# Token tiles transposed by a diagonal, gate weights asked for later, the pair list worked out after the first pair's rows, in a hybrid decoder step on one Trainium2 core

## The chip, the cores and the metric

The kernel is one launch on one NeuronCore of one Trainium2 chip. The metric is device microseconds from start to end of an execution. A profile of one execution by the hardware profiler comes beside the times.

## The reference

One layer of a hybrid decoder step over 536 tokens (16 meta tokens, 512 prompt tokens, 8 decode tokens), all in float32. Cut to what matters here:

```python
h = rms_norm(x, norm_mix)                      # x * rsqrt(mean(x*x) + eps) * g, 1024 wide
p = h @ w_in                                   # mlstm q,k,v,o, 8 gate columns, attention q,k,v
... mLSTM heads and differential attention heads ...
x = x + concat(heads) @ w_out
h = rms_norm(x, norm_ffn)
g_idx = argmax(softmax(h @ w_group + b_group))            # one of 4 groups
top_v, top_i = top_k(expert logits of that group, 2)      # two of its 8 experts
for e in range(32):
    act = silu(h @ w_gate[e]) * (h @ w_up[e])             # 1024 -> 256
    y  += gates[:, e] * (act @ w_down[e])                 # 256 -> 1024
out = rms_norm(x + y, norm_final)
```

## The kernel before, in words

Tokens lie in five tiles of rows: four of 128 prompt tokens, and one of 40 rows (`T4`) with the meta and decode tokens. A list `ORDER`, written out by the function `schedule`, gives the order of work items; each engine walks the same list and does its own part of each item, with semaphores between them. SyncE (SP) issues nearly all DMAs; ScalarE (ACT), VectorE (DVE) and GpSimd (POOL) each have their own strict order too.

The head. SP asks for token tiles 0 and 1 (512 KB each), the first block of `w_in` (2 MB), and the other tiles. ACT asks for `gmix`, and for the eight gate columns of `w_in` in two DMAs (lines 969 and 970) whose pieces are 16 bytes each, into `wg`; it then squares and sums each token tile (line 979). POOL turns the sum into the row's factor `rr` (lines 802, 804). DVE multiplies the whole tile by `rr` into `hn` (line 1371). TensorE (PE) transposes `hn` in eight 128-column pieces (item `xt`, line 1804), and DVE copies the result, times `gmix`, into `hT` (line 1235). The list begins with `xt` 0, `xt` 1, `acc dv 0` (eight k-steps of a 128x512 product, line 1867), then `xt` 2, `acc dv 1`, and so on, one tile's transposes between two products. After block `dv` come `dq` (line 1864), the item `gates` (line 1846, which needs `wg`), `dk`, `mqk` and the mixers.

The middle. For the channel mixer the tokens are gathered by expert. Items `rank` and `invert` find, by a chain of small DVE operations, the slots of the first three pairs of experts (`EARLY`), and POOL gathers their rows from the DRAM tensor `tok_rows` into `XG` (line 901). Item `order` then makes the full list of pairs; at its end `table_ready` lets SP look up the later experts, and twelve more small DVE operations (lines 1674 to 1686) work out where the later pairs' slots lie. DVE then does `rows_of(0)` (line 1719: copies the first pair's transposed rows, times `gffn`, into `xT`), `late_ids` (lines 1694 to 1702 and `place_rows`) and `late_rows`.

The experts. 32 experts are worked through as 16 pairs and one repeated turn (`TURNS`, 17 turns). Three sets of weight slots hold three pairs; 3 MB belong to one expert. In a turn PE multiplies by gate and up weights (`gate_up`, line 2132), transposes the next pair's rows (line 2124), multiplies by the down weights of the turn before (line 2145) and transposes the activations (line 2138). SP asks for a later pair's gate weights when `gate_filled` says that the set's gate weights were used (line 543 from `next_gate_up`), for its up weights after `gu_filled` (line 546), and for its down weights after `dn_filled` (line 549).

Of the kernel before, what the change touches and what calls it, by code (L numbers as in the profile page):

```python
# [7 lines left out]
D = 1024  # L8
# [7 lines left out]
H = 4  # L16
DQ = 64
DV = 128
NEXP = 32
# [3 lines left out]
KC = D // 128  # L23
# [10 lines left out]
NTILES = NT + 1  # L34


SLOTS = 64
# [12 lines left out]
NOROOM = 4096  # L50
# [163 lines left out]
def build(nc, x_prompt, x_sample, cache_k, cache_v, state_C, state_n, state_m, page_table, meta_tokens,  # L214
# [7 lines left out]
    with ctx:  # L222
# [3 lines left out]
        def sem(name):  # L226
            return ctx.enter_context(nc.semaphore(name))
# [73 lines left out]
        feat = {"dq": dqT, "dk": dkT, "mqk": mqkT}  # L301
        hn = [HO[:, 0, :], HO[:, 1, :]]

# [45 lines left out]
        sums_ready = sem("sums_ready")  # L349
        hn_ready = sem("hn_ready")  # L350
        act_step, dve_step, pool_step, sp_step = (sem(n) for n in ("act_step", "dve_step", "pool_step", "sp_step"))
# [96 lines left out]
        riota = sb("riota", [128, 128])  # L448
        piota = sb("piota", [128, NPAIRS])
        iscr = moflat[:, 0:128].bitcast(i32)  # L450
        eidx = sb("eidx", [128, 32])
# [506 lines left out]
        def _(act):  # L958
# [7 lines left out]
            act.dma_start(gmix[:, :], norm_mix[0].rearrange("(p k) -> p k", k=KC)).then_inc(gmix_in, 16)  # L966
            g = w_in[0].rearrange("(p k) n -> p k n", k=KC)[:, :, W_COLS["gates"]:W_COLS["gates"] + 8]
            act.wait_ge(wg_zeroed, 1)
            act.dma_start(wg[:, :, 0:H], g[:, :, 0:H]).then_inc(wg_in, 16)
            act.dma_start(wg[:, :, 32:32 + H], g[:, :, H:2 * H]).then_inc(wg_in, 16)  # L970

            act.wait_ge(ident_made, 1)
# [10 lines left out]
            for item in ORDER:  # L983
# [14 lines left out]
                elif kind == "acc":  # L998
                    b, m = item[1:]
                    after(act, item, "a%d" % (m % 2))  # L1000
                    src = PS["a%d" % (m % 2)]
# [208 lines left out]
        def _(dve):  # L1210
# [151 lines left out]
            for item in ORDER:  # L1362
                kind = item[0]
                if kind == "xt":
                    j = item[1]
                    n = nrows(j)

                    for i in ((0, 1) if j == 0 else (j + 1,) if j + 1 < NTILES else ()):
# [186 lines left out]
                elif kind == "logit":  # L1555
                    j = item[1]
                    n = nrows(j)
                    if j == 0:
                        link(v.memset(Lt[:, :, :], 0.0))
                        link(v.tensor_copy(trib, tri[:, :]))  # L1560
                        link(v.tensor_copy(onesb, ones[:, :]))
                        link(v.memset(e32[0], 1.0))
                        link(v.memset(MM[:, 160:192], 0.0))
                    dve.wait_ge(rsq, RSQ["wo", j, 1 if j < T4 else 0])
                    after(dve, item, "t")
                    v.scalar_tensor_tensor(Lt[0:n, j, :], PS["t"][0:n, 0:36], rr[0:n, 5 + j:6 + j], br[0:n, :],
                                           ALU.mult, ALU.add).then_inc(freed["t"], 1)
                elif kind == "rank":
# [33 lines left out]
                    for dst, o in ((M1, o1), (M2, o2)):  # L1602
# [27 lines left out]
                elif kind == "order":  # L1630
# [42 lines left out]

                    link(v.tensor_tensor(xs, xin, rest, ALU.subtract))
                    link(v.tensor_tensor(q, eidx[:, :], below, ALU.subtract))
                    link(v.tensor_scalar(u_, q, float(2 * FULL), 2.0, ALU.is_ge, ALU.mult))
                    link(v.tensor_tensor(q, q, u_, ALU.add))
                    link(v.scalar_tensor_tensor(pos, below, float(2 * FULL), q, ALU.add, ALU.subtract))
                    link(v.tensor_tensor(pos, pos, top, ALU.mult))
                    link(v.tensor_tensor(pos, pos, q, ALU.add))  # L1680

                    link(v.scalar_tensor_tensor(u_, xs, 2.0, below, ALU.add, ALU.subtract))
                    link(v.tensor_tensor(u_, u_, top, ALU.mult))
                    link(v.tensor_tensor(d2, u_, top, ALU.subtract))
                    link(v.tensor_tensor(d1, xs, u_, ALU.subtract))
                    link(v.scalar_tensor_tensor(d1, d1, float(NEXP + 1), pos, ALU.add, ALU.subtract))

# [29 lines left out]
            def rows_in(dst):  # L1717
                for half in range(2):
                    ins = v.tensor_tensor(dst[:, 4 * half:4 * half + 4, :],  # L1719
                                          bank[half][:, :].rearrange("p (k t) -> p k t", t=128),  # L1720
                                          gffn[:, 4 * half:4 * half + 4, None].to_broadcast([128, 4, 128]), ALU.mult)
                return ins
# [25 lines left out]

            rows_of(0)
            late_ids()  # L1750
            late_rows()
# [12 lines left out]
            def further_pair(i):  # L1764
                dve.wait_ge(xt_filled, i + STATIC)
                rows_in(xT[0]).then_inc(xt_evac, 1)
# [26 lines left out]
        def _(pe):  # L1793
            def transpose_rows(rows, item, j):
# [331 lines left out]

            def gate_up(gu, rows, w, due):
# [23 lines left out]
            def xt(i):  # L2151
                pe.wait_ge(xg_in[i % 2], 16 * (i // 2) + 16)
                if i:
                    pe.wait_ge(xt_evac, i)
                rows_out(XG[i % 2]).then_inc(xt_filled, 1)
# [14 lines left out]
            for i in range(STATIC):  # L2170
                s, n = i % 2, TURNS[i][0]
                w = 2 * (n % NSETS)
                pe.wait_ge(xt_evac, i + 1)
# [4 lines left out]
                gate_up(PS["t" if s else "p"], xT[s], w, 32 * (n // NSETS) + 32)  # L2178
                if i == 0:
# [12 lines left out]
            def further_pair(i):  # L2192
                pe.wait_ge(xg_in[0], 16 * i + 16 * ((STATIC + 1) // 2))
                rows_out(XG[0]).then_inc(xt_filled, 1)
                pe.wait_ge(xt_evac, i + STATIC)
                gate_up(PS["p"], xT[0], 0, 32 * i + 32 * ((PAIRS + NSETS - 1) // NSETS))
                pe.wait_ge(act_done, i + STATIC)
# [36 lines left out]
```

## Time and profile before

| | |
|---|---|
| median of 3 runs | 730.23 us (725.73 to 734.33) |
| the profiled execution, its own time | 722.13 us |
| its span, first to last instruction | 720.4 us |
| mean granted TensorE clock | 0.931 |
| PE busy | 612.6 us, 85% |
| DVE busy | 280.2 us, 39% |
| HBM read and written | 150.91 MB and 19.01 MB |

Times below are microseconds from the start of the span; durations are microseconds or, where so marked, ns. The profiled execution was quicker than the median of the timed ones by 8 us, so differences are worked out within it and then set on the median.

### The profile page before, as it was taken

How to read it: one execution, taken by the hardware profiler on the slowest of the kernel's cores; microseconds unless marked ns; L12 is line 12 of the kernel's file. 1: busy time of each engine (PE TensorE's matmuls, PEld its weight loads, DVE VectorE, ACT ScalarE, POOL GpSimd, SP SyncE). 2: the span in 40 equal slices, each digit the busy share in tenths (PEclk: the TensorE clock that was granted, in tenths of full speed). 3: DMA queues.
4: the chain of work that ended last, by engine and by line, in shares of the span. 5: the costliest groups of instructions: out<-in, count | busy, mean ns of one | idle time of the engine just before them, and what ended most of it. 6: DMA issues, size and time to landing. Idle time of an engine off the chain costs nothing.

```text
span 720.4 us, 8557 instructions
## 1 busy us (share of the span) xinstructions
PE 612.6 (85%) x3155; PEld 329.5 (46%) x3155; DVE 280.2 (39%) x615; ACT 139.3 (19%) x405; POOL 117.3 (16%) x195
## 2 busy tenths in 40 slices
PE   4999999898999898999999961899999877999700
PEld 2544344344545454555555541555556443554300
DVE  3220069422343333368976758512121211112046
ACT  3110052223233433321032010101010000101011
POOL 2340017200210101100022101111111111110023
PEclk9999999997999899999989975899999998999965
DMA  9643337813120300041019498799999999999674
GB/s 283 203 116 133 118 115 219 286 34 117 45 73 0 118 1 0 1 117 41 20 47 392 167 347 351 313 410 420 419 420 420 420 422 421 422 417 419 250 267 179
DMA packets 49378, 161.45 MB, mean 224 GB/s; under 512 B 16443, under 2 KB 17772, under 8 KB 36664
## 3 DMA queue, kind: packets, MB, share of 16 engines
q1 hardware_dynamic: 39624, 143.67, 51.8%
q0 software_dynamic: 7488, 17.19, 7.2%
q8 instruction: 26, 0.43, 0.2%
q10 hardware_dynamic: 2224, 0.04, 0.2%
q14 instruction: 16, 0.13, 0.0%
HBM read 150.91 MB, written 19.01 MB: 236 GB/s over the span
## 4 chain that ended last, share of the span: by engine, by line
PE 68%; DMA 14%; SPq 7%; DVE 6%; ACT 2%; issue 2%; POOL 1%; POOLq 0%; DVEq 0%; ACTq 0%
PE bank L1867 11%; PE bank L1864 10%; PE bank L2082 8%; PE bank_p L2132 6%; PE scores L2145 5%; DMA WS<-in_w_down_e 4%; DMA FT<-in_w_down_e 4%; PE bank_t L2132 4%; SPq L546 3%; PE bank_t L1881 2%; SPq L549 2%; PE bank_p L1990 2%; SPq L543 2%; PE scores L1958 2%; DMA WS<-in_w_in 2%
## 5 line engine op out<-in xcount | busy, mean ns | idle before, releaser
L1867 PE MATMUL bank<-WS,XHT 128*128 128x512 f32 x192 | 90.7, 621 | 1.3 <-DMA WS<-in_w_in 1.1
L1864 PE MATMUL bank<-XHT,WS 128*128 128x512 f32 x192 | 84.7, 597 | 0.3 <-PE bank_t L1881 0.3
L1867 PEld LDWEIGHTS bank<-WS,XHT 128*128 128x128 f32 x192 | 36.5, 199 | 43.7 <-issue 41.6
L1864 PEld LDWEIGHTS bank<-XHT,WS 128*128 128x128 f32 x192 | 35.8, 190 | 42.5 <-issue 42.3
L2132 PE MATMUL bank_p<-WS,XHT 128*64 128x256 f32 x288 | 45.4, 391 | 5.5 <-DVE XHT L1719 1.5
L911 POOL DMA_INDIRECT out_rows<-MVA,slot_ids x17 | 17.0, 1001 | 188.6 <-DVE MVA L1736 188.6
L2132 PE MATMUL bank_t<-WS,XHT 128*64 128x256 f32 x288 | 43.0, 381 | 2.0 <-DMA FT<-in_w_up_e 1.3
L802 POOL TENSOR_SCALAR rr<-ss 128x1 f32<-128x1 f32 (+3 forms) x25 | 7.8, 312 | 183.0 <-ACT XHT L1141 63.8
L2132 PEld LDWEIGHTS bank_p<-WS,XHT 128*64 128x64 f32 x288 | 27.8, 141 | 20.7 <-issue 4.0
L1736 DVE COPY MVA<-scores 128x512 f32<-128x512 f32 x17 | 11.8, 692 | 57.1 <-PE scores L2145 57.1
L2132 PEld LDWEIGHTS bank_t<-WS,XHT 128*64 128x64 f32 x288 | 26.4, 137 | 16.1 <-DMA FT<-in_w_up_e 1.8
L1478 DVE TENSOR_TENSOR scores<-scores,maskneg 128x256 f32<-128x256 f32 (+1 forms) x20 | 7.7, 383 | 63.1 <-PE scores L1961 63.1
L2082 PE MATMUL bank<-WS,FT 128*128 128x512 f32 x64 | 29.6, 606 | 0.0
L2145 PE MATMUL scores<-WS,FT 128*64 128x512 f32 x72 | 24.4, 675 | 6.1 <-DMA WS<-in_w_down_e 5.3
L2124 PE MATMUL bank<-ident,DVt 128*128 128x128 f32 x136 | 20.5, 296 | 10.4 <-DMA DVt<-tok_rows,slot_ids 10.4
L843 POOL DMA_INDIRECT MO<-in_cache_k,pages x16 | 17.6, 1102 | 68.9 <-DVE Sd L1432 51.3
L2082 PE MATMUL bank<-WS,XHT 128*128 128x512 f32 x64 | 28.7, 594 | 0.0
L1757 DVE TENSOR_TENSOR MVA<-DVt,bank_p 128x256 f32<-128x256 f32 x9 | 3.8, 422 | 62.9 <-ACT DVt L1182 62.9
L981 ACT ACTIVATE MVA<-scores 128x512 f32<-128x512 f32 x17 | 10.1, 597 | 87.2 <-PE scores L2145 87.2
L1757 DVE TENSOR_TENSOR MVA<-DVt,bank_t 128x256 f32<-128x256 f32 x8 | 3.4, 422 | 59.7 <-ACT DVt L1182 59.7
L804 POOL TENSOR_TENSOR rr<-rr,neghalf 128x1 f32<-128x1 f32 (+3 forms) x25 | 24.9, 995 | 2.1
L2124 PEld LDWEIGHTS bank<-ident,DVt 128*128 128x128 f32 x136 | 17.1, 196 | 16.2 <-issue 16.2
(421 smaller groups left out, 1025.5 us busy)
## 6 DMA issues: line engine op xcount, KB each, us to landing
WS<-in_w_gate_e SPq DMA_DIRECT2D x16, 1024.0 KB, 19.3
WS<-in_w_up_e SPq DMA_DIRECT2D x16, 1024.0 KB, 21.6
WS<-in_w_down_e SPq DMA_DIRECT2D x16, 1024.0 KB, 24.9
WS<-in_w_in SPq DMA_DIRECT2D x6, 2048.0 KB, 11.8
XHT<-in_w_gate_e SPq DMA_DIRECT2D x10, 1024.0 KB, 22.5
XHT<-in_w_up_e SPq DMA_DIRECT2D x10, 1024.0 KB, 24.7
XHT<-in_w_down_e SPq DMA_DIRECT2D x10, 1024.0 KB, 26.3
FT<-in_w_gate_e SPq DMA_DIRECT2D x6, 1024.0 KB, 23.4
```

The source lines that it names most:

```text
L543: sp.dma_start(Wgu[w][:, 0], w_gate_e[0, e].rearrange("(p k) n -> p k n", k=KC)).then_inc(gate_in[w // 2], 16)
L546: sp.dma_start(Wgu[w][:, 1], w_up_e[0, e].rearrange("(p k) n -> p k n", k=KC)).then_inc(up_in[w // 2], 16)
L549: sp.dma_start(Wdn[w], w_down_e[0, e].rearrange("(p f) n -> p f n", f=FC)).then_inc(dn_in[w // 2], 16)
L804: pool.tensor_tensor(dst, dst, neghalf[0:dst.shape[0], 0:n], ALU.pow).then_inc(rsq, 1)
L843: pool.indirect_dma_start(dst, None, cache[0].rearrange("n t h d -> (n t) (h d)"), bass.IndirectOffsetOnAxis(ap=pages[:, b * NPAGES + p:b ...
L911: pool.indirect_dma_start(out_rows, bass.IndirectOffsetOnAxis(ap=slot_ids[:, c, 1:2].bitcast(u32), axis=0), YO[s], None, bounds_check=2 * ...
L1864: mm = pe.matmul(PS[r][:, :], w[:, k, 128 * m:128 * (m + 1)], hT[:, k, 0:512], start=(k == 0), stop=(k == KC - 1))
L1867: mm = pe.matmul(PS[r][:, :], hT[:, k, 128 * m:128 * (m + 1)], w[:, k, :], start=(k == 0), stop=(k == KC - 1))
L2082: mm = pe.matmul(PS[b][0:n, :], rows[:, k, col(j):col(j) + n], blkslot[(6 + half) % 3][:, first + k, :], start=(k == 0), stop=(k == 3))
L2124: mm = pe.transpose(bank[k // 4][:, 128 * (k % 4):128 * (k % 4) + 128], src[:, k:D:KC], ident[:, :])
L2132: mm = pe.matmul(gu[64 * u:64 * u + 64, DE * g:DE * g + DE], rows[:, k, 64 * u:64 * u + 64], Wgu[w + u][:, g, k, :], start=(k == 0), stop= ...
L2145: mm = pe.matmul(Sps[64 * u:64 * u + 64, 0, 512 * half:512 * half + 512], act_t[:, f, 64 * u:64 * u + 64], Wdn[w + u][:, f, 512 * half:512 ...
```

## The change

1. `hn` is gone. DVE makes a 128x128 diagonal `rrdiag` (the identity times the rows' factors), and PE multiplies the raw tile `X` by it, piece by piece: an ordinary float32 matmul in place of a transpose, for all five tiles of item `xt`. The transposes of `rt` and of the experts stay as they are.
2. The two DMAs for `wg` are issued by ACT when it comes to `acc dq 1`, not at the start.
3. In `rank` two small DVE operations of the chain go (the offset `NOROOM` is folded into constants that two operations at `logit 0` make).
4. The twelve operations after `table_ready` become `pair_places`, called after `rows_of(0)`.
5. `rows_in` signals `xt_evac` after each of its two halves, and `gate_up` waits for the first half before k-step 0 and for the second before k-step 4. The waits that count `xt_evac` count twice as far.

```diff
-        hn = [HO[:, 0, :], HO[:, 1, :]]
+        rrdiag = [HO[:, 0, 128 * n:128 * n + 128] for n in range(2)]
...
+        early_rows, early_pairs = Wd[:, 0, 0:2 * EARLY], Wd[:, 1, 0:EARLY]
...
-            act.wait_ge(wg_zeroed, 1)
-            act.dma_start(wg[:, :, 0:H], g[:, :, 0:H]).then_inc(wg_in, 16)
-            act.dma_start(wg[:, :, 32:32 + H], g[:, :, H:2 * H]).then_inc(wg_in, 16)
...
+                    if (b, m) == ("dq", 1):
+                        act.wait_ge(wg_zeroed, 1)
+                        act.dma_start(wg[:, :, 0:H], g[:, :, 0:H]).then_inc(wg_in, 16)
+                        act.dma_start(wg[:, :, 32:32 + H], g[:, :, H:2 * H]).then_inc(wg_in, 16)
...
-                        v.tensor_scalar(hn[i % 2][0:n], X[0:n, i, :], rr[0:n, i:i + 1], None, ALU.mult).then_inc(hn_ready, 1)
+                        v.tensor_scalar(rrdiag[i % 2][0:n, 0:n], ident[0:n, 0:n], rr[0:n, i:i + 1], None, ALU.mult).then_inc(rrdiag_made, 1)
...
+                        v.tensor_scalar(early_rows[:, :], eidx[:, 0:2 * EARLY], float(SLOTS), float(-NOROOM), ALU.mult, ALU.add)
+                        link(v.tensor_scalar(early_pairs[:, :], piota[:, 0:EARLY], float(-NOROOM), None, ALU.add))
...
-                    link(v.scalar_tensor_tensor(early, eidx[:, None, 0:ne].to_broadcast([128, NTILES, ne]), float(SLOTS), early,
-                                                ALU.mult, ALU.add))
-                    link(v.tensor_scalar(early, early, float(-NOROOM), None, ALU.add))
+                    link(v.tensor_tensor(early, early, early_rows[:, None, :].to_broadcast([128, NTILES, ne]), ALU.add))
...
-                    link(v.tensor_scalar(slot_of, slot_of, float(NOROOM), None, ALU.add))
-                    place_rows(first_onehots, piota[:, 0:EARLY])
+                    place_rows(first_onehots, early_pairs[:, :])
...
+            def pair_places():
...   (the twelve operations, unchanged)
             rows_of(0)
+            pair_places()
             late_ids()
...
-                rows_in(xT[s]).then_inc(xt_evac, 1)
+                rows_in(xT[s])          # .then_inc(xt_evac, 1) on each half, inside
...
+                        if g == 0 and k % 4 == 0:
+                            pe.wait_ge(xt_evac, evacuated + (1 if k else 0))
...
-                        mm = pe.transpose(dst[:, 128 * k:128 * k + n], rows[0:n, 4 * half + k:D:KC], ident[0:n, 0:n])
+                        if scaled is None:
+                            mm = pe.transpose(out, src, ident[0:n, 0:n])
+                        else:
+                            mm = pe.matmul(out, src, scaled[0:n, 0:n], start=True, stop=True)
...
-                    pe.wait_ge(hn_ready, j + 1)
-                    transpose_rows(hn[j % 2], item, j)
+                    pe.wait_ge(rrdiag_made, j + 1)
+                    transpose_rows(X[:, j, :], item, j, rrdiag[j % 2])
```

## Rows read from the trace of the kernel before

**Rows 1.** The chain that ended last, in order of time: start us, us, what; head.

```profile
1.72 11.55 DMA WS<-in_w_in
13.31 8.77 PE bank L1867 x16
22.08 0.88 PE scores L1804 x8
22.96 6.87 PE bank L1867 x16
```

**Rows 2.** Timeline of the head: start, us, engine, line, what, [idle before <-releaser].

```profile
2.89 0.29 POOL L778 TENSOR_SCALAR_AFFINE_SELECT ident<-ident 128x128 f32<-128x128 f32 x1 [0.24 <-POOL ident L777]
...
3.80 1.28 ACT L973 ACT_TABLE_LOAD   x1 [3.80 <-issue]
...
7.62 0.75 DVE L1371 TENSOR_SCALAR XHT<-XHT,rr 128x1024 f32<-128x1024 f32 x1 [4.46 <-POOL rr L804]
...
8.52 3.65 PE L1804 MATMUL scores<-ident,XHT 128*128 128x128 f32 x16 [8.52 <-DVE XHT L1371]
```

**Rows 3.** DMA queues in the first 13.3 us: packets, MB, share of 16 engines.

```profile
q10 hardware_dynamic: 1091, 0.02, 4.9%
```

**Rows 4.** Groups of instructions, whole span, shapes apart: xcount | busy us, mean ns.

```profile
L1990 PE MATMUL bank_p<-DVt,WS 128*128 128x128 f32 x80 | 14.5, 316 | 0.0
...
L1975 PE MATMUL bank_t<-ident,WS 128*128 128x128 f32 x40 | 8.1, 308 | 0.0
```

**Rows 5.** The chain again: one head's product by the values, in mid-kernel.

```profile
267.25 1.10 PE bank_p L1990 x8
```

**Rows 6.** Groups on DVE, shapes apart: a 128x128 product with a column.

```profile
L1422 DVE TENSOR_SCALAR gda<-gda 128x128 f32<-128x128 f32 x1 | 0.2, 227 | 0.0
```

**Rows 7.** The tile wg: time of its two DMAs from issue to landing.

```profile
DMA to landing us min/median/max: 13.9/16.8/19.6
```

**Rows 8.** ACT's timeline in block dq, and the chain at the gates.

```profile
56.69 0.60 ACT L981 ACTIVATE FT<-bank 128x512 f32<-128x512 f32 x1 [6.64 <-PE bank L1864]
...
82.63 7.03 PE bank_t L1846 x16
```

**Rows 9.** DVE's timeline at rank and at the pair list.

```profile
434.34 0.18 DVE L1615 TENSOR_SCALAR MO<-MO 128x30 f32<-128x30 f32 x1
...
447.64 0.19 DVE L1674 TENSOR_TENSOR MO<-MO 128x32 f32<-128x32 f32 x1
...
450.13 0.19 DVE L1686 SCALAR_TENSOR_TENSOR MO<-MO 128x32 f32<-128x32 f32 x1
...
451.00 1.29 DVE L1719 TENSOR_TENSOR XHT<-bank,gffn 128x512 f32<-128x512 f32 x2 [0.68 <-PE bank L2124]
...
457.10 1.48 DVE L1349 TENSOR_TENSOR MVA<-riota,MO 128x1280 bf16<-128x1280 f32 x1
```

**Rows 10.** The chain from the first gather to the second turn.

```profile
440.25 8.56 DMA DVt<-tok_rows,slot_ids
...
452.34 9.41 PE bank_p L2132 x64
461.82 1.28 ACT L1182
...
465.20 7.13 PE bank_t L2132 x64
```

**Rows 11.** Busy time by stretch: us, PE, PEld, DVE, ACT, POOL, PEclk, DMA share, GB/s.

```profile
456.00:458.00 2.00, 2.00 (x18) 1.20 (x16) 1.93 (x5) 0.00 (x0) 0.00 (x0) 0.76 0.05 14
...
470.00:475.00 5.00, 5.00 (x38) 2.89 (x36) 1.71 (x3) 0.38 (x1) 0.00 (x0) 1.00 0.99 400
...
640.00:660.00 20.00, 20.00 (x162) 12.12 (x158) 2.90 (x6) 1.90 (x5) 3.02 (x3) 1.00 1.02 421
```

**Rows 12.** SP's issues of gate weights in the first two turns.

```profile
458.48 0.36 SPq L543 DMA_DIRECT2D WS<-in_w_gate_e  x1
...
469.07 0.85 SPq L543 DMA_DIRECT2D WS<-in_w_gate_e  x2
```

More of the change, by code:

```diff
@@ L349, in build @@
         sums_ready = sem("sums_ready")
-        hn_ready = sem("hn_ready")
+        rrdiag_made = sem("rrdiag_made")
         act_step, dve_step, pool_step, sp_step = (sem(n) for n in ("act_step", "dve_step", "pool_step", "sp_step"))
@@ L966, in _ @@
             act.dma_start(gmix[:, :], norm_mix[0].rearrange("(p k) -> p k", k=KC)).then_inc(gmix_in, 16)
-            g = w_in[0].rearrange("(p k) n -> p k n", k=KC)[:, :, W_COLS["gates"]:W_COLS["gates"] + 8]
-            act.wait_ge(wg_zeroed, 1)
-            act.dma_start(wg[:, :, 0:H], g[:, :, 0:H]).then_inc(wg_in, 16)
-            act.dma_start(wg[:, :, 32:32 + H], g[:, :, H:2 * H]).then_inc(wg_in, 16)
             act.wait_ge(ident_made, 1)
@@ L999, in _ @@
                     b, m = item[1:]
+                    if (b, m) == ("dq", 1):
+                        g = w_in[0].rearrange("(p k) n -> p k n", k=KC)[:, :, W_COLS["gates"]:W_COLS["gates"] + 8]
+                        act.wait_ge(wg_zeroed, 1)
+                        act.dma_start(wg[:, :, 0:H], g[:, :, 0:H]).then_inc(wg_in, 16)
+                        act.dma_start(wg[:, :, 32:32 + H], g[:, :, H:2 * H]).then_inc(wg_in, 16)
                     after(act, item, "a%d" % (m % 2))
@@ L1366, in _ @@
                     n = nrows(j)
+                    if j == 0:
+                        dve.wait_ge(ident_made, 1)
                     for i in ((0, 1) if j == 0 else (j + 1,) if j + 1 < NTILES else ()):
@@ L1672, in _ @@
                     v.nop().then_inc(table_ready, 1)
[L1674 to L1686, printed above, removed]
+            def pair_places():
+                one32, extra, key, key2, top, incl, below, rest, xin, xs, pos, d1, d2, q, u_ = e32
+                link(v.tensor_tensor(xs, xin, rest, ALU.subtract))
+                link(v.tensor_tensor(q, eidx[:, :], below, ALU.subtract))
+                link(v.tensor_scalar(u_, q, float(2 * FULL), 2.0, ALU.is_ge, ALU.mult))
+                link(v.tensor_tensor(q, q, u_, ALU.add))
+                link(v.scalar_tensor_tensor(pos, below, float(2 * FULL), q, ALU.add, ALU.subtract))
+                link(v.tensor_tensor(pos, pos, top, ALU.mult))
+                link(v.tensor_tensor(pos, pos, q, ALU.add))
+                link(v.scalar_tensor_tensor(u_, xs, 2.0, below, ALU.add, ALU.subtract))
+                link(v.tensor_tensor(u_, u_, top, ALU.mult))
+                link(v.tensor_tensor(d2, u_, top, ALU.subtract))
+                link(v.tensor_tensor(d1, xs, u_, ALU.subtract))
+                link(v.scalar_tensor_tensor(d1, d1, float(NEXP + 1), pos, ALU.add, ALU.subtract))
             def late_ids():
@@ L1718, in rows_in @@
                 for half in range(2):
[L1719 to L1722, printed above, removed]
+                    v.tensor_tensor(dst[:, 4 * half:4 * half + 4, :],
+                                    bank[half][:, :].rearrange("p (k t) -> p k t", t=128),
+                                    gffn[:, 4 * half:4 * half + 4, None].to_broadcast([128, 4, 128]),
+                                    ALU.mult).then_inc(xt_evac, 1)
             def rows_of(i):
@@ L1765, in further_pair @@
                 dve.wait_ge(xt_filled, i + STATIC)
-                rows_in(xT[0]).then_inc(xt_evac, 1)
+                rows_in(xT[0])
                 dve.wait_ge(silu_done, i + STATIC)
@@ L1793, in _, with transpose_rows @@
         def _(pe):
-            def transpose_rows(rows, item, j):
+            def transpose_rows(rows, item, j, scaled=None):
                 n = nrows(j)
@@ L1803, in transpose_rows @@
                     for k in range(4):
-                        mm = pe.transpose(dst[:, 128 * k:128 * k + n], rows[0:n, 4 * half + k:D:KC], ident[0:n, 0:n])
+                        src, out = rows[0:n, 4 * half + k:D:KC], dst[:, 128 * k:128 * k + n]
+                        if scaled is None:
+                            mm = pe.transpose(out, src, ident[0:n, 0:n])
+                        else:
+                            mm = pe.matmul(out, src, scaled[0:n, 0:n], start=True, stop=True)
                     if len(names) == 2 or half == 1:
@@ L2125, in rows_out, with gate_up @@
                 return mm
-            def gate_up(gu, rows, w, due):
+            def gate_up(gu, rows, w, due, evacuated):
                 for g, (loaded, done) in enumerate(((gate_in, gate_filled), (up_in, gu_filled))):
@@ L2153, in xt @@
                 if i:
-                    pe.wait_ge(xt_evac, i)
+                    pe.wait_ge(xt_evac, 2 * i)
                 rows_out(XG[i % 2]).then_inc(xt_filled, 1)
@@ L2172, in _ @@
                 w = 2 * (n % NSETS)
-                pe.wait_ge(xt_evac, i + 1)
                 if i >= 2:
@@ L2177, in _ @@
                     pe.wait_ge(ids_ready, 2)
-                gate_up(PS["t" if s else "p"], xT[s], w, 32 * (n // NSETS) + 32)
+                gate_up(PS["t" if s else "p"], xT[s], w, 32 * (n // NSETS) + 32, 2 * i + 1)
                 if i == 0:
@@ L2194, in further_pair @@
                 rows_out(XG[0]).then_inc(xt_filled, 1)
-                pe.wait_ge(xt_evac, i + STATIC)
-                gate_up(PS["p"], xT[0], 0, 32 * i + 32 * ((PAIRS + NSETS - 1) // NSETS))
+                gate_up(PS["p"], xT[0], 0, 32 * i + 32 * ((PAIRS + NSETS - 1) // NSETS), 2 * i + 2 * STATIC - 1)
                 pe.wait_ge(act_done, i + STATIC)
```

## The prediction

> **What bounds the kernel now.** I read the chain of waits in order of time first, to see which waits stand where the change works, then the timeline and the DMA queues there, and last the busy time by stretch. PE is TensorE throughout. In the head the chain runs over the landing of the first `w_in` block: asked for at 1.72, it lands at 13.27, and `acc dv 0` starts at 13.31 and takes 8.77 us, where the same sixteen instructions take 6.87 us in the next product [rows 1]. From 22.08 on the chain is PE without a gap, transposes and products in turn, so what PE gains or loses in the head goes to the end of the router, through waits that PE itself sets off. In the middle the chain is the small DVE operations of `rank`, the gather of the first pair (8.56 us), its transposes, one evacuation and the first `gate_up` [rows 9, 10]. From 459 on the DMA queue is what counts. It stands idle from 456 to 458 (share 0.05), and from SP's issue at 458.48 on it runs at 0.99 to 1.02 of its time, about 421 GB/s, up to the last down weights [rows 11]. So after 459 PE's own time is worth nothing, and the end moves by as much as the issue at 458.48 moves, which is released by the gate half of turn 0 [rows 12].
>
> **The change part by part.**
>
> *Diagonal, tiles 2 to 4 (a loss).* An ordinary float32 product is two PE instructions where a transpose is one: the product by the values has 10 blocks and 4 heads, 40 calls, and shows 80 instructions; the transposes of the same 40 blocks show 40 [rows 4]. Eight instructions of 128 columns take 0.88 us as transposes [rows 1] and 1.10 us as parts of ordinary products, the first one's start-up in it [rows 5]. A tile goes from 8 instructions to 16, so it costs 0.88 us more (1.10 at most). Tiles 2, 3 and 4 stand in the gapless stretch: 3 x 0.88 = 2.64 us more, up to 3.3. Nothing hides it; DVE's 0.75 us for `hn` that goes is hidden there already.
> The Trainium skill ("TensorE: Matmul & The Clock Gate", section "Terms") has the transpose mode 4 times faster for float32; here the rows give 2 times. By the page each tile would cost three times 0.88 us more, not once.
>
> *Diagonal and gate weights, tiles 0 and 1 (a gain).* Today ACT loads its table for 1.28 us from 3.80, behind its two wg issues, then squares tile 0, and PE starts at 8.52 [rows 2]. Without the issues the table load can start once POOL's identity is there, at 3.2 to 3.3 [rows 2], so tile 0 is squared about 0.5 us sooner (between 0, if the tile's landing sets it, and 1.1 us, if the load doesn't wait for the identity). DVE's 0.75 us [rows 2] becomes a 128x128 product, 0.23 us [rows 6]: 0.5 us. PE starts at about 7.4. It then has 32 instructions, not 16; at the 228 ns of today (3.65 / 16 [rows 2]) they end at 14.7, later than today's 12.17.
> But the clock moves too. Sixteen instructions take 8.77 us in `dv 0` and 6.87 after it [rows 1]; at 429 ns each, doubled while the clock is at 1.2 GHz, 1.9 us too much means that it rose 3.8 us after the products began. Turn 0 takes 9.41 us against 7.13 [rows 10]: by the same sum it rose about 4.6 us after they began (granted 0.76 of full speed over 456 to 458 [rows 11]). If the diagonal products, which are ordinary ones, count the same, the clock is at 2.4 GHz 3.8 to 4.6 us after 7.4, at 11.2 to 12.0. By 11.6 PE has done 18.6 of the 32; 13.4 x 0.110 = 1.5 us more, and it is ready at 13.1.
> The block's landing: the wg pieces took 4.9% of the engines' first 13.3 us [rows 3], 0.65 us, so it lands at about 12.6 (12.6 to 13.3). The later of the two is 13.1. From there `dv 0` takes 6.87 and ends at 20.0, not 22.08: 2.1 us gained. Bounds: 2.6 gained (landing 12.6, clock up), 1.4 lost (ready at 14.7, 8.77 as today: ends at 23.47).
> The same page ("Part 4: PE-mode transpose") says that transposes do not count as busy for the clock gate. The sixteen transposes before `dv 0` did not leave a raised clock behind them [rows 1, 2], which fits; if they did count, the diagonal brings the clock nothing, and the first rival below is the case.
> Head in sum: 2.64 - 2.1 = 0.55 us slower.
>
> *wg later, at the gates.* ACT issues both behind the eviction of `dq 0`, at 57.3; it has nothing else until 63 [rows 8], so nobody queues behind it. The longest landing of before is 19.6 us, in a crowded queue [rows 7]: 57.3 + 0.8 + 19.6 = 77.7, and PE comes to the gates at 82.63 [rows 8]. Cost nothing, with 4.9 us of cover.
>
> *rank.* Two operations go, L1615 (0.18 us [rows 9]) and its like at L1618, with 0.03 to 0.04 us to the next start: 0.41 us off the chain to the gather. The gather takes 8.56 us and shares its queue with weights, so 0 to 0.41 comes through; DMA was nearly idle at its end, I take 0.41. The two added operations at `logit 0` run in a stretch where DVE waits for PE: nothing.
>
> *Half signals.* PE starts turn 0 after the first half of the evacuation, 1.29 / 2 = 0.65 us sooner. With rank 1.06 us sooner in all, at the low clock: if the clock then rises just as much sooner, 1.06 us reach the issue at 458.48; if it rises at the same moment as today, half, 0.53. I take 0.8. In later turns the evacuation lies beside the down product: nothing.
>
> *pair_places moved.* It brings no gain: today DVE has done the twelve operations at 450.32 and waits until 451.00 for PE's transposes [rows 9], so `rows_of(0)` wasn't held up. It costs its 2.68 us (447.64 to 450.32) in `late_ids`. Today that ends its one-hots at 457.10 + 1.48 = 458.58 [rows 9]; now at 458.58 + 2.68 - 0.41 = 460.9, with a gap or two more 461.0. PE ends turn 0's `gate_up` at 461.75 today (452.34 + 9.41 [rows 10]), now at 460.7 to 461.2. So PE's search for the later rows waits 0.3 us at most, DVE's slot ids come about when the first SiLU does (ACT loads a table for it, 1.28 us [rows 10]), and turn 1 starts near 464.1 against 465.20 [rows 10]. That is off the DMA chain: the wait is covered by the queue's work.
>
> **Sum.** +2.64 - 2.1 - 0.8 = -0.25 us on the profiled execution's 722.13: 721.9. The median of before is 8.1 us above that execution; set on it, 730.0 us. About 1% (7.3 us) is what a measurement of this kernel can tell from no change, and this is far inside.
>
> **The rivals.**
> 1. *The diagonal does not raise the clock sooner (slower).* PE is ready at 14.7 and `dv 0` takes 8.77 again: +1.4 + 2.64 - 0.8 = +3.2, 733.5 us. For it: the clock stayed low through the transposes before `dv 0`, and what counts for its rise shows only with wide products here. Against: turn 0's products have half the array's columns each and raised it. It decides as soon as the rise comes after 14.7.
> 2. *All of the head's gain comes (faster).* `dv 0` at 12.6, 1.06 us through to the queue, and turn 1's earlier gate weights fill the small gap at 470 to 475 (400 against 421 GB/s, 0.25 us [rows 11]): -2.6 + 2.64 - 1.06 - 0.25 = -1.3, 728.9 us.
> 3. *The later pair list surfaces.* Turn 1 waits for `ids_ready`, and SP's issue at 469.07 waits for turn 1's gate half. The 4 MB asked for from 458.48 on last 10 us at 421 GB/s, to about 468.6, so a later issue there leaves the queue empty. It decides when turn 1 starts after 465.2, 1.1 us later than worked out; at most 2.68 - 1.1 = 1.6 us, 731.6 us.
> 4. *The change does not do what it says at the gates:* wg lands over 25 us after its issue and PE waits there, some 1 us: 731.
> 5. *A plain product costs four transposes.* By rows as a mechanism: 64 instructions in tiles 0 and 1, ready at 11.6 + 45.4 x 0.11 = 16.6, `dv 0` ends at 23.5 (+1.4), tiles 2 to 4 cost 7.9: +8.5 with the middle's gain, 738.7. The counts in [rows 4] speak against it. The skill's page on TensorE is cited for this above.
>
> **How the numbers follow.** Forecast 0.45, its own range 729.2 to 731; rival 1 0.22, rival 2 0.17, rival 3 0.06, rival 4 0.03, rival 5 0.03, something else 0.04. The cases that hold most lie between 728.9 and 733.5. Three runs of one kernel spread from 725.73 to 734.33, which is wider than all terms here together, so a median of a few runs may lie 3 us off: 725.5 to 735. Faster by over 1% needs something not seen here: 0.03. Slower by over 1% is rival 5 and a part of the unknown: 0.05. Within 1%: 0.92.
>
> **What would show it.** L1804's successor shows 16 instructions a tile for `xt` at 110 to 137 ns each. The first product starts near 13.1, takes 6.9 us and ends near 20; if it takes 8.8, rival 1 is right. PE reaches `dq` 0.5 us later than 49.54, and the gates without a wait for wg. The first gather is issued at the same distance less 0.4 us from the last logit. Turn 0 starts about 0.65 us after its evacuation began. The twelve operations stand behind the evacuation, and PE waits under 0.3 us for the one-hots. SP's first gate issue of turn 0 comes about 0.25 us sooner than 458.48. The prediction is wrong if the gather or a landing in the decode part answers to the shift by more than the shift itself, or if the DMA stage is not bound by its bytes.

## The result: 1.5% slower, outside the predicted range

| | before | after |
|---|---|---|
| median of the runs on one chip, us | 730.01 (718.12 to 734.33, 22 runs) | 738.73 (728.53 to 745.13, 22 runs) |
| ratio, 95% interval | | 1.0154 (1.0108 to 1.0199) |
| profiled execution, its span, us | 722.13, 720.4 | 736.17, 734.3 |
| PE busy us, mean granted clock | 612.6, 0.931 | 627.2, 0.929 |

730.0 (725.5 to 735) was forecast; the medians lie 8.7 us apart. The medians here and below are over all runs of a kernel, the ratios over its fast runs alone (those within 1.5% of its fastest), so a ratio can differ from that of the medians: 1.0154 is 11.2 us. The head of the changed kernel's chain of waits, in order of time (start us, us, what), answers to [rows 1]:

```profile
0.79 3.44 DMA XHT<-in_x_prompt
4.31 1.16 ACT WS L975 x2
...
7.06 7.89 PE scores L1814 x32
14.95 6.87 PE bank L1877 x16
21.82 3.68 PE scores L1814 x16
...
42.91 3.92 PE scores L1814 x16
46.84 8.73 PE bank L1877 x16
55.57 3.61 PE bank_t L1891 x32
59.47 27.71 PE bank L1874 x64
...
92.55 7.03 PE bank_t L1856 x16
```

Read it downwards. The products by the diagonal (L1814) start at 7.06, 1.46 us sooner than the transposes of [rows 2], and `acc dv 0` takes 6.87 us, not 8.77: the clock is up when it begins (the trace's first record of full clock stands at 12.6, before at 16.6; ahead of a trace's first record its clock column reads 1.00 and says nothing). It begins at 14.95, though, not 13.31, since the 32 products before it last 7.89 us. Then each of tiles 2 to 4 takes 3.68 to 3.92 us where eight transposes took 0.88 to 1.00. The line at 46.84 is a third thing: `dv 3` takes 8.73 us, where 7.06 were taken before. Stretch by stretch (window, its length, busy time of each engine, granted clock, DMA share, GB/s), the clock fell right behind tile 4:

```profile
43.00:46.80 3.80, 3.80 (x17) 3.75 (x17) 0.00 (x0) 0.55 (x1) 0.00 (x0) 0.99 0.00 0
46.80:50.50 3.70, 3.70 (x6) 1.67 (x6) 3.11 (x12) 0.00 (x0) 1.95 (x2) 0.55 0.16 18
50.50:55.50 5.00, 5.00 (x13) 1.90 (x11) 0.77 (x4) 0.00 (x0) 3.26 (x11) 1.00 0.72 198
```

The account up to `dq`, which starts at 59.47 against 49.54: `dv 0` ends 0.26 sooner (21.82 against 22.08); tiles 2 to 4 cost 2.80, 2.80 and 2.92 more, 8.52; `dv 3` at the low clock costs 8.73 - 7.06 = 1.67. Together +9.93, which is the whole distance. The gates stand at the same +9.92, with no wait for wg.

The middle, on the same chain, answers to [rows 9, 10]:

```profile
442.83 0.26 DVE Lt L1571
...
455.38 8.54 DMA DVt<-tok_rows,slot_ids
...
466.03 1.29 DVE XHT L1724 x2
```

And PE's timeline there ([idle before <-releaser]):

```profile
466.87 0.66 PE L2144 MATMUL bank_p<-WS,XHT 128*64 128x256 f32 x1 [0.87 <-DVE XHT L1724]
...
476.38 0.42 PE L1822 MATMUL bank_t<-MVA 128*128 128x48 bf16 x10 [0.86 <-DVE MVA L1350]
```

Before, the last logit stood at 427.27, so the gather came 12.98 us behind it; now 12.55: 0.43 sooner. Turn 0 follows the start of its evacuation by 0.84 us, not 1.34, and stands 1.04 us nearer to the last logit. PE waits 0.86 us for the later rows' one-hots.

So the profiles show +9.93 at `dq` and -1.04 at turn 0: +8.9, beside 8.7 between the medians and 11.2 by the ratio. Between `dq` and the last logit this execution lost 5.6 us more; the experiments say whose those are.

### The profile page after: what moved, and what is told of

Its sections match the earlier page's. It is cut to its first block, busy times and chain, and to the rows that moved or that the text cites. A ratio compares the mean times of both kernels' runs of the same rounds, so it can differ in the third digit from the quotient of the medians.

```text
span 734.3 us, 8636 instructions
## 1 busy us (share of the span) xinstructions
PE 627.2 (85%) x3195; PEld 344.7 (47%) x3195; DVE 277.6 (38%) x615; ACT 139.3 (19%) x405; POOL 115.1 (16%) x195
## 3 DMA queue, kind: packets, MB, share of 16 engines
HBM read 150.91 MB, written 19.01 MB: 231 GB/s over the span
## 4 chain that ended last, share of the span: by engine, by line
PE 63%; DMA 12%; SPq 11%; DVE 7%; issue 2%; ACT 2%; POOL 1%; POOLq 0%; DVEq 0%; ACTq 0%
PE bank L1877 11%; PE bank L1874 10%; PE bank L2092 8%; SPq L547 4%; DMA WS<-in_w_down_e 4%; DMA FT<-in_w_down_e 4%; SPq L550 4%; PE scores L2157 3%; PE bank_p L2144 3%; PE bank_t L2144 3%; SPq L544 3%; PE scores L1814 3%; PE bank_p L2000 2%; PE bank_t L1891 2%; PE scores L1968 2%
## 5 line engine op out<-in xcount | busy, mean ns | idle before, releaser
L1877 PE MATMUL bank<-WS,XHT 128*128 128x512 f32 x192 | 92.4, 630 | 0.1
L844 POOL DMA_INDIRECT MO<-in_cache_k,pages x16 | 16.6, 1039 | 80.7 <-DVE Sd L1435 54.0
L2092 PE MATMUL bank<-WS,XHT 128*128 128x512 f32 x64 | 28.7, 594 | 0.0
L2157 PE MATMUL scores<-WS,MK 128*64 128x512 f32 x72 | 23.6, 624 | 2.7 <-DMA FT<-in_w_down_e 2.7
L2157 PE MATMUL scores<-WS,FT 128*64 128x512 f32 x72 | 21.9, 597 | 4.6 <-DMA WS<-in_w_down_e 3.8
L1814 PE MATMUL scores<-XHT 128*128 128x128 f32 (+1 forms) x80 | 19.6, 412 | 7.1 <-DVE XHT L1374 7.1
## 6 DMA issues: line engine op xcount, KB each, us to landing
WS<-in_w_in SPq DMA_DIRECT2D x6, 2048.0 KB, 11.3
```

Of the source, the lines that this page charges most:

```text
L844: pool.indirect_dma_start(dst, None, cache[0].rearrange("n t h d -> (n t) (h d)"), bass.IndirectOffsetOnAxis(ap=pages[:, b * NPAGES + p:b ...
L1814: mm = pe.matmul(out, src, scaled[0:n, 0:n], start=True, stop=True)
L1877: mm = pe.matmul(PS[r][:, :], hT[:, k, 128 * m:128 * (m + 1)], w[:, k, :], start=(k == 0), stop=(k == KC - 1))
L2092: mm = pe.matmul(PS[b][0:n, :], rows[:, k, col(j):col(j) + n], blkslot[(6 + half) % 3][:, first + k, :], start=(k == 0), stop=(k == 3))
L2157: mm = pe.matmul(Sps[64 * u:64 * u + 64, 0, 512 * half:512 * half + 512], act_t[:, f, 64 * u:64 * u + 64], Wdn[w + u][:, f, 512 * half:512 ...
```

## The experiments

Theory A, held from here on: an ordinary float32 product whose operand has its columns eight numbers apart, as `rows[0:n, 4 * half + k:D:KC]` has, costs about 230 ns for 128 columns (3.68 / 16) and not the 110 ns of the transposes, and this is the loss. Rivals: every ordinary product on tiles costs it (rival 5 of the prediction), the middle costs it, or the clock does.

**e1: the products by themselves.** Groups of ordinary products (two instructions each) and of transposes, behind wide products that hold the clock at full speed. It computes nothing of the step.

```
for k in range(16): pe.matmul(out, A[:, k % 8:1024:8], ident, ...)     # L290; L281: contiguous
for k in range(16): pe.transpose(out, A[:, k % 8:1024:8], ident)       # L299
for k in range(16): pe.matmul(out, ident, A[:, k % 8:1024:8], ...)     # L305: the moving operand
```

> A kernel of its own that computes nothing of the step: TensorE alone, groups of sixteen 128x128 float32 operations behind eight 128x512 products each. Ordinary products by the identity with the stationary operand's columns 1, 2, 4, 8 and 16 floats apart; transposes with the same operand contiguous, 8 and 16 apart; and products with the identity stationary and the moving operand 8 apart and contiguous. Theory A (the column step of the stationary operand of an ordinary float32 product sets the time): 110 to 115 ns an instruction at step 1, 230 at step 8, with the step from one to the other somewhere between; transposes 110 at every step; the moving operand's step costs nothing. Theory B (an ordinary product of a token tile by a 128x128 square is slow in any layout): 230 ns at step 1 too, or at least over 180.

Its timeline on PE:

```profile
15.75 3.73 PE L281 MATMUL q<-ident,A 128*128 128x128 f32 x32
...
36.82 7.50 PE L287 MATMUL q<-ident,A 128*128 128x128 f32 x32
...
51.03 7.65 PE L290 MATMUL q<-ident,A 128*128 128x128 f32 x32
...
65.39 7.04 PE L293 MATMUL q<-ident,A 128*128 128x128 f32 x32
...
79.13 1.91 PE L296 MATMUL q<-ident,A 128*128 128x128 f32 x16
...
87.75 1.94 PE L299 MATMUL q<-ident,A 128*128 128x128 f32 x16
...
105.06 7.62 PE L305 MATMUL q<-A,ident 128*128 128x128 f32 x32
```

and the groups of two of its lines, for the loads of the stationary operand (PEld) and the products (xcount | busy us, mean ns of one):

```profile
L290 PEld LDWEIGHTS q<-ident,A 128*128 128x128 f32 x32 | 7.8, 334 | 0.4 <-issue 0.2
...
L305 PEld LDWEIGHTS q<-A,ident 128*128 128x128 f32 x32 | 6.6, 207 | 1.2 <-issue 0.5
...
L281 PEld LDWEIGHTS q<-ident,A 128*128 128x128 f32 x32 | 3.7, 192 | 0.5 <-issue 0.5
```

Divide each group by its count: step 1 gives 117 ns, step 2 (3.92 us for 32) 122, step 4 (L287) 234, step 8 (L290) 239, step 16 (L293) 220. The transposes take 119 contiguous, 121 at step 8 and 123 at step 16. Theory A holds, with one miss: I had expected the moving operand to be free of it, and it costs 238 ns too. The loads suggest that the price sits in the instruction that reads the wide-stepped tile: the load takes 334 ns instead of 192 in L290, and 207 in L305, where the stationary operand is contiguous. In the changed kernel the loads of L1814 take 335 ns (median), in e5 192.

**e3 and e2: the diagonal alone, and everything but the diagonal.** e3 is the kernel before with the diagonal's edits; e2 is the changed kernel with the scaled copy and the transposes back:

```diff
-                        v.tensor_scalar(rrdiag[i % 2][0:n, 0:n], ident[0:n, 0:n], rr[0:n, i:i + 1], None, ALU.mult).then_inc(rrdiag_made, 1)
+                        v.tensor_scalar(hn[i % 2][0:n], X[0:n, i, :], rr[0:n, i:i + 1], None, ALU.mult).then_inc(rrdiag_made, 1)
...
-                    transpose_rows(X[:, j, :], item, j, rrdiag[j % 2])
+                    transpose_rows(hn[j % 2], item, j)
```

> The kernel before with part 1 alone. If the diagonal products are the loss: 8 to 11 us slower than before, ratio 1.011 to 1.015, dq starting 8 us or more later than 49.5. If the loss came from an interplay with the other parts: under 4 us slower.

> The changed kernel with part 1 undone: the scaled copy hn and transposes, all else of the change kept. If the diagonal products are the whole loss (3 x 2.8 us in tiles 2 to 4, 8.4 us in all): the gate weights' absence from the head, the shorter rank chain and the half signals are left, 1 to 2.5 us faster than the kernel before: ratio 0.9965 to 0.999. If something else in the change costs (pair_places later, gate weights later): slower than before by over 2 us.

e3 took 740.74 us against 726.97, ratio 1.0237 (1.0168 to 1.0306); e2 725.67, ratio 1.0028 (0.9991 to 1.0065). The loss goes with the diagonal: it is there in e3 and not measurable in e2. Neither ratio fell into the expected range, though. e2 should have come out faster than before and did not; by its interval up to 0.65% could still be the other parts'. e3 lost 13.8 us and not 8 to 11, 5 more than the changed kernel. It lacks that kernel's two gains: PE starts at 8.07, not 7.06, and turn 0 stands as far behind the last logit as before. That is 2 us; the other 3 are open. e3's chain has the same three things, the low clock behind tile 4 too:

```profile
8.07 7.89 PE scores L1810 x32
...
22.82 3.68 PE scores L1810 x16
...
43.92 3.93 PE scores L1810 x16
47.84 8.76 PE bank L1873 x16
```

In e2, `dv 0` is the line to read, from PE's timeline:

```profile
7.55 3.65 PE L1810 MATMUL scores<-ident,XHT 128*128 128x128 f32 x16 [7.55 <-DVE XHT L1372]
13.15 7.13 PE L1875 MATMUL bank<-WS,XHT 128*128 128x512 f32 x16 [1.95 <-DMA WS<-in_w_in]
```

There are only transposes ahead of it, as in the kernel before, and yet it takes 7.13 us, not 8.77: the first record of full clock stands at 11.2 in this trace, where the transposes end. So `dq` comes at 47.76, 1.8 us sooner than before, of which 0.16 is the earlier start and the rest the clock. Its turn 0 stands 1.05 us nearer to the last logit. Neither shows in its time.

**e4 and e5: the same products on neighbouring columns.** e4 is the changed kernel, reading 128 neighbouring columns of `X`. The features then stand in another order than the weights' rows, so the step's numbers are others:

```diff
+                        if scaled is not None:
+                            src = rows[0:n, 128 * (4 * half + k):128 * (4 * half + k) + 128]
```

> The changed kernel, but the pieces of X that PE multiplies by the diagonal are 128 neighbouring columns, not every eighth: the features come out in another order, so the numbers computed are others; sizes and counts are the same. Theory A: an instruction of L1814 takes 110 to 115 ns, a tile 1.8 us in place of 3.7, dq starts 5.5 us or more sooner than in the changed kernel, about level with the kernel before (ratio 0.997 to 1.003, as predicted blind). Theory B: no difference from the changed kernel, ratio 1.012 to 1.018. The routing of tokens changes with the numbers, so the expert stage may differ a little.

Its head did what was expected (1.78 us a tile, `dq` at 50.41), but its time, 767.92 us, ratio 1.0598, tells nothing: with other numbers the router chose other experts, and more was to be loaded and computed (157.72 MB read from HBM, not 150.91). e5 mends that by loading `w_in`, the gate weights and `gmix` in the same order, `"(k p) n -> p k n"` in place of `"(p k) n -> p k n"`, so that it computes the same thing as the reference.

> The changed kernel with the features dealt to the partitions the other way round: piece k of X is its 128 neighbouring columns, and the blocks of w_in, the gate weights and gmix are loaded to match, so the result is the reference's. Sixteen instructions a tile as in the change, stationary columns next to each other. Theory A (the step of 8 floats in an ordinary float32 product is what costs): a tile takes 1.8 us, dq starts within 1.5 us of 49.5, the whole within 3 us of the kernel before (ratio 0.996 to 1.004), 8 to 12 us faster than the changed kernel. If the diagonal costs for another reason that the bench does not have: ratio above 1.01.

725.95 us against 724.28, ratio 1.0013 (0.9973 to 1.0054). Its chain:

```profile
7.29 6.38 PE scores L1816 x32
13.67 6.87 PE bank L1879 x16
20.54 1.78 PE scores L1816 x16
...
37.84 1.91 PE scores L1816 x16
39.75 7.06 PE bank L1879 x16
...
50.71 27.70 PE bank L1876 x64
```

With the step gone, each of tiles 2 to 4 costs 0.90 us more than as transposes, `dq` stands 1.17 us later than before, and no low clock follows tile 4. This is the kernel that the blind sum described.

**e8: the diagonal for tiles 0 and 1 only,** where PE would otherwise wait for the weights; tiles 2 to 4 as scaled copies and transposes.

> The changed kernel with the diagonal for tiles 0 and 1 alone, transposes of a scaled copy for tiles 2 to 4. The 8.4 us of the three later tiles go; dv 0 starts near 15 as in the changed kernel but at the high clock, so dq starts near 49.3, 1.5 us later than with transposes throughout. Ratio to the kernel before 0.997 to 1.002. If it stays above 1.01, the loss is not in the later tiles' products.

```profile
15.21 6.87 PE bank L1883 x16
22.07 0.88 PE scores L1815 x8
...
38.58 7.06 PE bank L1883 x16
...
49.55 27.70 PE bank L1880 x64
```

`dv 0` starts 1.90 us later and takes 1.90 less: `dq` stands at 49.55, as in the first profile of before (49.54). Against that profile the whole loss of the head comes with the products of tiles 2 to 4, the low clock behind tile 4 included. Ratio 0.997 (0.9923 to 1.0016), as expected.

**e6, e7, e11: the middle in parts.** e6 is the kernel before with the changes to `rank`, the half signals and the pair list. e7 is e2 with the pair list back ahead of `rows_of(0)`. e11 is the kernel before with the pair list alone moved (`pair_places()` behind `rows_of(0)`).

> The kernel before with parts 3, 4 and 5 alone (shorter rank chain, pair_places later, half signals). Theory A: first gate issue of turn 0 comes 0.8 to 1.8 us sooner after the last logit, head unchanged; ratio 0.997 to 0.999. Rival (the moved pair list surfaces): turn 1 starts later after the last logit than before and the ratio is above 1.001.

> Transposes kept, parts 2, 3 and 5 kept, pair_places put back before rows_of(0). The twelve operations then stand where DVE waits over 3 us for PE's transposes; turn 0 starts as soon and the search for the later rows no longer waits (0.9 us in the changed kernel). If that wait reached the DMA queue: up to 1 us faster than with the list moved; if not, the same. Against the kernel before: ratio 0.995 to 1.001.

> The kernel before with part 4 alone: the twelve operations of the pair list behind the evacuation of the first pair's rows. By the blind sum it is neutral: the evacuation starts at the same distance from the last logit (within 0.1 us), PE waits 0 to 0.9 us for the later rows' one-hots, SP's first gate issue keeps its distance from the last logit, ratio 0.997 to 1.003. Rival 3 (the later list surfaces): turn 1 starts later by 1.1 us or more against turn 0, the queue falls empty before turn 1's gate weights, ratio 1.001 to 1.003 and the share of the DMA engines dips between turn 0 and turn 1.

| | us | against before | turn 0 from the last logit |
|---|---|---|---|
| e6 | 726.95 | 1.0049 (1.0018 to 1.008) | -1.25 us |
| e7 | 724.45 | 0.9995 (0.9952 to 1.0038) | -0.79 us |
| e11 | 728.94 | 1.0017 (0.9954 to 1.008) | -0.34 us |

The list moved alone costs nothing that can be seen: the distance between turns 0 and 1 grew by 0.21 us, not by the 1.1 from which rival 3 decides, and the DMA engines are at 1.00 of their time from 465 to 471.9, where turn 1's weights are asked for. The gain of the middle is in the profiles of e6 and e7, but in no ratio. e6 was expected to be faster (0.997 to 0.999) and comes out a little slower, which is open. Its ratio is the one named for the rival, but turn 1 doesn't start later, as the rival wants: it stands 36.12 us behind the last logit, 37.93 before. The profile has `dv 0` at 10.07 us, with the first full clock at 19.8, in a head that was not edited.

**e9 and e10: both kernels once more,** for what belongs to a run.

> The kernel before once more, with a profile of its own, to see which differences between two profiles come from run to run. If the stretches in which the granted clock is low between the block dq and the mixers' end belong to the run and not to the kernel, they lie elsewhere than in the first profile (171 to 181, 242 to 249, 365 to 372, 416 to 423 us) and add up to 3 to 8 us of shift at the last logit. If they belong to the kernel, they stand within 1 us of the same places. Either way dv 0 starts at 13.1 to 13.4 and no low stretch stands at 40 to 51 us.

> The changed kernel once more. Theory A (the step of eight in the products is the whole loss): each of tiles 2 to 4 again takes 3.6 to 3.9 us, dq starts 8 us or more after that of before. The drop of the clock after tile 4's products (from 47.0 in the first profile) stands again within 1 us if it belongs to these products; if it was a run's chance it is absent, and dq starts at 57.6 instead of 59.5. The last logit comes 8 to 10 us later than in the kernel before if the further 6 us of the first profile were drops of the run.

e10's chain in the head repeats that of the changed kernel to 0.05 us:

```profile
42.94 3.96 PE scores L1814 x16
46.90 8.68 PE bank L1877 x16
...
59.48 27.70 PE bank L1874 x64
```

So the drop of the clock behind tile 4 belongs to the kernel. The clock in `dv 0` is the run's, as long as transposes stand ahead of it. e9, whose `dv 0` starts at 13.68 and not at the expected 13.1 to 13.4, had it up at 11.3 and lost it again within `dv 0`, from 14.8 on:

```profile
15.10:18.50 3.40, 3.40 (x6) 1.34 (x5) 1.18 (x2) 2.27 (x4) 0.74 (x2) 0.55 1.07 260
```

Over all profiles of this study with transposes there, `dv 0` took 8.77 (before), 8.83 (e9), 10.07 (e6) and 7.13 us (e2, e7 and e11); with the diagonal at step 8 6.87 us in each of four (after, e10, e3, e8), with contiguous columns 7.13 and 6.87 (e4, e5).

What comes after `dq` differs by the run too. From `dq` to the last logit the kernel before took 377.7 us in its first profile and 384.6 in e9 (49.99 to 434.60), the changed kernel 383.4 and then 376.2. One kernel differs from itself there by 7 us. The places of the low clock are neither within 1 us of the first profile's nor altogether elsewhere: counted from `dq`, four of its five come again 1 to 8 us later in e9, one does not, and two are new. The clock is low for 31.8 us of this stretch in the first profile and 41.0 in e9 (mean granted 0.96 and 0.95), for 37.7 and then 23.9 in the changed kernel (0.95 and 0.97). At half clock at most half of such time is lost, so this covers 4.6 of the 6.9 us and 6.9 of the 7.2; the rest is open. The 5.6 us that the first pair of profiles had there are therefore not shown to be an effect of the change. Over all profiles this stretch took between 374.9 (e5) and 387.5 us (e4). That places e9 correctly as well: 729.92 us, with nothing changed, 7.8 above the first profiled execution.

**e12: narrower tiles, and the steps between.** Like e1; L281 has a stationary step of 3, L284 and L287 a moving step of 2 and 4, L290 and L293 products of 40 rows and 40 columns at step 8 (tile 4's shape), L296 the same contiguous; L274 are the wide products between, 7.03 to 7.05 us at full clock. It computes nothing of the step.

> It computes nothing of the step: ordinary float32 products by themselves on TensorE, each group behind eight wide products. Theory A (one operand whose columns lie 16 bytes or more apart costs double): stationary operand with step 3: 112 to 120 ns an instruction; moving operand with step 2: 112 to 120; with step 4: 225 to 235. Rival (the moving operand pays at any step): step 2 at 150 ns or more. Last, 40 rows by 40 columns with a stationary step of 8, as tile 4 has it: if few rows make it cheaper, below 150 ns an instruction; in the changed kernel they took 245. If such products do not hold the clock up, the granted clock falls behind the long run of 96 of them and the wide products after it take about 859 ns instead of 429; if the drop in the changed kernel had another cause, it stays at full speed.

```profile
15.69 5.68 PE L281 MATMUL q<-ident,A 128*128 128x128 f32 x32
...
38.57 7.41 PE L287 MATMUL q<-A,ident 128*128 128x128 f32 x32
...
52.79 7.83 PE L290 MATMUL q<-ident,A 40*128 40x40 f32 x32
60.54 9.82 PE L274 MATMUL acc<-B 128*128 128x512 f32 x16
70.29 23.05 PE L293 MATMUL q<-ident,A 40*128 40x40 f32 x96
93.27 8.82 PE L274 MATMUL acc<-B 128*128 128x512 f32 x16
102.02 3.76 PE L296 MATMUL q<-ident,A 40*128 40x40 f32 x32
105.71 8.83 PE L274 MATMUL acc<-B 128*128 128x512 f32 x16
```

Step 3 takes 178 ns, which theory A had at 112 to 120: the price comes in two steps, at 3 and at 4, and not at 4 alone. A moving step of 2 takes 118 (3.79 us for 32), of 4 232, as expected. The 40x40 products take 245 ns at step 8, as many as the full tile, and 118 contiguous. The wide products behind each 40x40 group are slow (9.82, 8.82, 8.83 us against 7.05), behind the contiguous group too: behind these small products the clock falls, whatever their step. And by stretch of the clock:

```profile
60.50:70.30 9.80, 9.80 (x18) 0.72 0.01 2
70.30:93.30 23.00, 23.00 (x98) 0.55 0.00 0
```

The 96 products ran at 240 ns each with the clock granted at 0.55: half TensorE's clock made the stepped products no slower. What limits them here is not TensorE's clock.

## Why the prediction was wrong

**The step that failed** is the first term, "Diagonal, tiles 2 to 4 (a loss)", where it took 0.88 us a tile, "1.10 at most". It measured 2.80, 2.80 and 2.92: 8.5 us and not 2.64. The count of instructions was right (16 for 8). The price of one was taken from the transposes of the same tile and from [rows 5], where both operands are contiguous. Neither row bounds an ordinary product that reads columns eight apart: transposes do not pay for the step (e1) and the rows of [rows 5] have none. The upper bound of 3.3 us came from a row that shared the shape and the type, but not the access. 5.9 us of the miss are here. With 1.8 us in tiles 0 and 1 and 1.7 us of low clock behind tile 4 (both below), less 0.2 us more gained in the middle than was counted, this makes 9.2, and the difference of the medians, 8.7, lies 9.0 us from the forecast one, -0.25.

**Tiles 0 and 1** were forecast 2.1 us sooner and came 0.26 sooner (0.0 in e8). PE's start was right: 7.4 forecast, 7.06 seen, since the table load begins at 1.24, ahead of the identity and not behind it. But PE was ready at 14.95, where 13.1 was forecast. In e5 it was ready at 13.67, after 6.38 us for the 32 instead of 7.89, so 1.5 us are the step again and the rest is the clock, up 5.6 us after PE's start and not 3.8 to 4.6. The block's landing was off too: forecast at 12.6 without the wg pieces, it came at 12.87 to 13.10 where PE waited for it (e7, e4, e2), and at 13.27 to 13.79 with them (before, e11, e9, e6). So even with contiguous columns the diagonal made PE ready too late for it (13.67 in e5).

`dv 0` took 6.87 us, as forecast, and rival 1 gave 8.77: it did not happen. The reason that I gave is not borne out, however. I had read from one profile [rows 1, 2] that the sixteen transposes leave the clock low, and counted 1.9 us as the diagonal's gain. In e2 and e7 it was up at 11.2 and 11.4, with nothing but transposes behind it, and three of six profiles with transposes have `dv 0` at 7.13. The rule that I took from the Trainium skill for this ("TensorE: Matmul & The Clock Gate", "Part 4: PE-mode transpose": transposes don't count as busy) does not agree with e2's 11.2. What the diagonal can be credited with is that `dv 0` was never slow in six profiles; against a run like e2 that is worth nothing, and the diagonal's head then costs not 9.93 but 11.7 us (59.47 against 47.76).

**The clock behind tile 4** was in no step: 1.67 us, in all three profiles with the diagonal at step 8 on tile 4 (after, e3, e10) and in none without. Tile 4 with its 40 rows keeps PE on small products for 3.9 us; contiguous it takes 1.91 (e5) and the clock holds there. Tiles 2 and 3, as long but 128 rows high, have no low clock behind them, and in e12 it falls behind 40x40 products.

**The middle** was right in size at turn 0: 1.06 us forecast, 1.04 seen (0.89 in e10, while e9, with nothing changed, stands 0.21 further off); for `rank` 0.41 and 0.43, for the half signals 0.65 and 0.50. PE waits 0.86 us for the one-hots, not 0.3 at most, but turn 1 starts no later for it. Rival 3 is refuted by e11. SP's first gate issue came 1.8 us nearer to the last logit in this profile, beyond the forecast 0.8, since the clock rose sooner within turn 0 here (3.1 us after its start, before 4.6); in e10 it is 1.56 (3.2), in e7 0.45 (5.3), so this size changes from run to run, or with the start, and I can't say which. From that issue on the first two profiles are alike: 262.0 us to the end before, 262.1 after, as the prediction had it, but 263.1 in e7 and 265.4 in e10. That the gain reaches the end was not shown: e2 and e7 are not faster than before.

**wg later** cost nothing, with far more cover than I gave it: the two DMAs, issued at 66.6 and 67.3, landed within 5.7 us, not the 19.6 of [rows 7].

**Rival 5** gave 738.7 and the median is 738.73, but its mechanism is wrong. It said that a plain product costs four transposes, in instructions. e5 shows two: 1.78 us for a tile against 0.88. The number agrees by luck: its sum has 1.4 us lost before tile 2 that did not come, and lacks the 1.67 of the low clock. The four of this kernel (3.68 / 0.88 = 4.2) are twice as many instructions, each twice as long through the step. The Trainium skill's 4 times for float32 ("TensorE: Matmul & The Clock Gate", section "Terms"), weighed in the prediction, so agrees in size with what the stepped tiles show here and not with the contiguous ones. That the Trainium skill spoke for a number outside my bounds was worth more than 0.03: no row of the kernel before showed an ordinary product with stepped columns, so the trace could not speak against it.

**What stays open:** why the ratio of e6 is above 1, why e3 lost 3 us more than its head accounts for, and whether the 1 us of the middle reaches the end. e2's profile gains 2.8 us in the head and the middle, but 1.6 of these are the clock of that one run, and between `dq` and the last logit it loses 3.8 again, within what one kernel differs from itself there. No version here is measurably faster than the kernel before.

## What to carry to other kernels

When a transpose is turned into an ordinary product, look at how the operand is read, not only at shape, type and count: in an ordinary product here a stationary float32 operand with its columns three numbers apart cost one and a half times the time and one with four or more about twice, a moving one with four or eight twice as well, and transposes at steps 8 and 16 paid nothing of it. Bound an unknown cost by rows that share the access pattern too, and where no row does, say that the bound is open. A clock that one profile shows low is a fact of that run until a second profile of the same kernel shows it there: here a term of 1.9 us rested on it, and one kernel differed from itself by 7 us.

## What was unexpected of the hardware

- The step of the stationary operand's columns: 117 ns (1), 122 (2), 178 (3), 234 (4), 239 (8), 220 (16) for an ordinary 128x128 float32 instruction; transposes 119 to 123 at steps 1, 8 and 16.
- At step 8 the time hangs neither on the tile's rows and columns (245 ns for 40x40) nor on TensorE's clock (240 ns with 0.55 granted).
- With sixteen transposes as PE's only work so far, the clock was full before the first wide product in some runs (first record at 11.2, 11.4, 11.3, 12.8) and not in others (16.6, 19.8), with PE's first instruction at 7.55 to 8.53 in all.
- Behind 3.76 us of 40x40 products between wide ones the clock fell; the next sixteen wide instructions took 8.83 us instead of 7.05.
